# Final norm and delta-layer norm: x times both weights as the projections' operand, token factors applied at the projections' evictions

## The reference, cut to what matters

```python
# end of the first block
x = x + gt2[:, None, :] * y              # y: output of the experts
x = rmsnorm(x, g_final)                  # x * rsqrt(mean(x*x) + eps) * g
# start of the second block (h is x)
h = h + deltanet_mixer(rmsnorm_2(h, a_norm[i]), a_w_in[i], a_conv_w[i], ...)

def deltanet_mixer(h, w_in, conv_w, A_log, dt_bias, onorm_g, w_out):
    p = h @ w_in                         # 1024 -> 3072 (q, k, v) + 1024 (gate) + 16
    qkv, gate, b_raw, a_raw = jnp.split(p, [...], axis=-1)
    qkv = jax.nn.silu(causal_dwconv_2(qkv, conv_w))     # 4 taps along the tokens
    q, k, v = jnp.split(qkv, [A_QK, 2 * A_QK], axis=-1)
    q = l2norm(q.reshape(...)) * (A_DK ** -0.5)
    k = l2norm(k.reshape(...))
    beta = jax.nn.sigmoid(b_raw)
    g = -jnp.exp(A_log) * jax.nn.softplus(a_raw + dt_bias)
    o = gated_delta_rule_chunked(q, k, v, beta, g)
    o = rmsnorm_2(o, onorm_g) * jax.nn.silu(gate)
    return o @ w_out
```

## Time and profile before

| | |
|---|---|
| runs of the kernel | 2513.53, 2516.08, 2520.11 us; median 2516.08 |
| profiled execution | 2513.93 us, span 2512.2 us |
| busy share of the span | TensorE 91%, VectorE 48%, ScalarE 32%, GpSimd 5% |
| transposes of the expert sum start | 1084.48 us |
| tile 0 of the projections | 1135.59 us |
| first matmul of the delta rule | 1341.25 us |
| the casts of `wab`, VectorE (L2069, L2070) | 0.22 and 0.29 us, at 1105.23 |
| first two units of weights, issued at 1066.2 and 1066.7 | land after 15.0 and 19.4 us |
| a unit of weights (2 MB), median of 63 | lands after 8.1 us |

### The profile page before, as it was taken

How to read it: one execution, slowest core, us unless ns; L and a number is a source line. 1 busy time by engine, 2 the same in 40 slices (tenths; PEclk the granted TensorE clock), 3 DMA queues, 4 the chain that set the end, 5 groups by cost and what they waited for, 6 DMA issues and landing times.

```text
span 2512.2 us, 29683 instructions
## 1 busy us (share of the span) xinstructions
PE 2288.1 (91%) x11716; PEld 1574.4 (63%) x11716; DVE 1193.6 (48%) x1734; ACT 813.6 (32%) x1250; POOL 119.8 (5%) x160
## 2 busy tenths in 40 slices
PE   7999898599999999839988589999999889999997
PEld 3778656333333333317767577888787777888775
DVE  4889575300000000055645544777824473777832
ACT  4222452311111111143365164232324274223322
POOL 0000000111111111100002000000000000000000
PEclk9999999799999999969989599999999899999999
DMA  9442205449999999521110001222222301222221
GB/s 368 159 167 76 91 1 235 167 188 376 373 380 396 392 386 380 216 121 68 67 67 34 1 34 67 101 100 100 101 89 79 134 1 67 101 100 86 81 101 67
DMA packets 36405, 384.54 MB, mean 153 GB/s; under 512 B 10080, under 2 KB 10336, under 8 KB 13408
## 3 DMA queue, kind: packets, MB, share of 16 engines
q1 hardware_dynamic: 27520, 374.91, 38.1%
q0 software_dynamic: 8800, 8.45, 1.0%
HBM read 384.10 MB, written 16.83 MB: 160 GB/s over the span
## 4 chain that ended last, share of the span: by engine, by line
PE 55%; DVE 16%; ACT 5%; issue 3%; DMA 1%; DVEq 0%; POOL 0%; ACTq 0%; SPq 0%; POOLq 0%
PE PS L591 9%; PE PS L592 9%; PE PS L593 9%; PE PS L793 9%; PE PS L832 4%; PE PS L813 4%; DVE ring_r L2039 3%; PE PS L840 2%; DVE A L1755 2%; ACT w_hi_r L1378 2%; PE PS L557 2%; DVE A L2249 1%; DVE hid_r L2262 1%; DVE sq L2247 1%; DVE A L2250 1%
## 5 line engine op out<-in xcount | busy, mean ns | idle before, releaser
L592 PE MATMUL PS<-h_r,w_hi_r 128*128 128x512 f32 x1104 | 432.5, 392 | 0.0
L591 PE MATMUL PS<-h_hi_r,w_hi_r 128*128 128x512 f32 x1056 | 417.8, 396 | 10.6 <-ACT A L1405 7.2
L593 PE MATMUL PS<-h_hi_r,ring_r 128*128 128x512 f32 x1056 | 413.5, 392 | 0.0
L2039 DVE TENSOR_TENSOR ring_r<-ring,w_hi_r 128x1024 fp32r<-128x1024 f32 x196 | 238.6, 1223 | 361.7 <-ACT w_hi_r L1378 361.7
L1378 ACT ACTIVATE w_hi_r<-ring 128x1024 fp32r<-128x1024 f32 x196 | 202.6, 1051 | 331.2 <-PE PS L593 204.2
L591 PEld LDWEIGHTS PS<-h_hi_r,w_hi_r 128*128 128x128 f32 x1056 | 199.7, 189 | 62.6 <-issue 17.4
L592 PEld LDWEIGHTS PS<-h_r,w_hi_r 128*128 128x128 f32 x1104 | 209.1, 189 | 45.0 <-issue 1.9
L593 PEld LDWEIGHTS PS<-h_hi_r,ring_r 128*128 128x128 f32 x1056 | 199.5, 189 | 42.0
L2015 DVE TENSOR_TENSOR A<-A,PS 128x512 f32<-128x512 f32 x16 | 11.0, 688 | 395.2 <-PE PS L793 395.2
L793 PE MATMUL PS<-A 128*64 128x512 f32 x768 | 169.2, 597 | 0.1
L591 PE MATMUL PS<-x_r,top_r 128*128 128x512 f32 x320 | 129.0, 403 | 12.6 <-DVE ring_r L1665 12.6
(11 more groups left out here) (447 smaller groups left out, 3741.6 us busy)
## 6 DMA issues: line engine op xcount, KB each, us to landing
A<-wexp SPq DMA_DIRECT2D x64, 2048.0 KB, 12.5
ring<-wall SPq DMA_DIRECT2D x63, 2048.0 KB, 8.1
ring<-wexp SPq DMA_DIRECT2D x16, 2048.0 KB, 18.8
h<-wexp SPq DMA_DIRECT2D x16, 2048.0 KB, 13.3
A<-wada SPq DMA_DIRECT2D x12, 2048.0 KB, 13.5
x<-xt_in SPq DMA_DIRECT2D x2, 2048.0 KB, 11.3
A<-y_assignments SPq DMA_DIRECT2D x4, 1024.0 KB, 7.9
h_tokens<-A SPq DMA_DIRECT2D x4, 512.0 KB, 2.8
```

The source lines that it names most:

```text
L591: mm(out, w[0], x_[0], start=first, stop=False)
L592: mm(out, w[0], x_[1], start=False, stop=False)
L593: return mm(out, w[1], x_[0], start=False, stop=last_)
L2039: tt(ring_r[:, slot, :, cols], ring[:, slot, :, cols], w_hi_r[:, :, cols].bitcast(F32), ALU.subtract).then_inc(S("w_lo"), 1)
```

## The change

The projections' operand becomes x times both norms' weights, g_final and a_norm, without any factor of the token. It is split into high part (ScalarE) and low part (VectorE) tile by tile, right as x is updated. Both norms' factors are per token, so they can be applied to the projections' outputs: `token_scale` is the product of norm 3's factor and norm 2's, and every output tile is multiplied by it when it leaves PSUM. For q, k and v that is one multiply into SBUF ahead of the convolution, which then reads SBUF; for the gate tiles VectorE multiplies and ScalarE applies Silu in place; for the 16 gate values it takes the place of a copy. Norm 2 still writes x, and norm 3 still takes its squares from that x. TensorE does tile 0, the gate values' product, norm 2's sums, tiles 1 and 2, norm 3's sums, tile 3. The sums go to banks 5 and 6. ScalarE and VectorE do the weight pieces and norms in the same order. The split of `wab` moves ahead of the update of x.

```diff
--- before.py
+++ after.py
@@ -89,7 +89,7 @@
 
 GROUPS = ([([f"in{i}"], "A") for i in range(10)] + [(["conv_out"], "D")] * 2 + [(["m_out"], "D")] * 2
           + [(["w_out0"], "X"), (["w_out1"], "X")]
-          + [([f"a_in{i}"], "D" if i < 6 else "A") for i in range(8)] + [(["a_out0"], "X"), (["a_out1"], "X")]
+          + [([f"a_in{i}"], "D") for i in range(8)] + [(["a_out0"], "X"), (["a_out1"], "X")]
           + [([f"up0_{i}"], "D") for i in range(FU)] + [([f"down0_{3 * m + i}" for i in range(3)], "X") for m in range(2)]
           + [(["kv"], "D"), (["w_q0"], "D"), (["w_q1"], "D"), (["w_o0"], "X"), (["w_o1"], "X")]
           + [([f"up1_{i}"], "D") for i in range(FU)] + [([f"down1_{3 * m + i}" for i in range(3)], "X") for m in range(2)])
@@ -276,6 +276,7 @@
         o_sum, o_std = [sb(f"o_{n}", [P, NT, DH]) for n in ("sum", "std")]
         l_sum = [A[:, u, :] for u in (24, 25, 26, 27, 28, 29, 54, 55, 56, 57, 58)] + [rstd[:]] + [A[:, u, :] for u in (24, 25, 26, 27)]
         g_last = ab[:, :, 0:DH]
+        token_scale = A[:, 23, :]
 
 
         moe_up, moe_dn = [A[:, 0:8], A[:, 32:40]], [A[:, 24:32], h[:]]
@@ -527,7 +528,7 @@
             for u in range(UIDX["down1_0"], NU):
                 load(u)
 
-            sp.wait_ge(S("h"), 32)
+            sp.wait_ge(S("h"), 24)
             sp.dma_start(out_t, h[:]).then_inc(S("out"), 16)
             sp.wait_ge(S("out"), 16)
 
@@ -847,8 +848,6 @@
                 for t in range(NT):
                     last = nc.tensor.transpose(PS[:, k, t * P:(t + 1) * P], A[:, 16 + 2 * t + k // 4, (k % 4) * P:(k % 4 + 1) * P], ident)
                 last.then_inc(S("yT"), 1)
-            norm(2, 0)
-
 
             def w_split(slot, k, cols):
                 return w_hi_r[:, k, cols], ring_r[:, slot, k, cols]
@@ -903,14 +902,26 @@
                     last.then_inc(S("mm"), 1)
 
 
-            norm(3, 0)
-            wait_split(1)
-
+            def a_tile(j):
+
+                pe.wait_ge(S("w_lo"), split_count(NU1, j))
+                for k in range(KD):
+                    if j == 0:
+                        pe.wait_ge(S("h_lo"), KD * (1 + MIX_SETS) + k + 1)
+                    last = product(PS[:, j, :], w_split(unit_slot(UNITS[NU1]), k, slice(j * P, (j + 1) * P)), h_split(k), k == 0, k == KD - 1)
+                last.then_inc(S("mm"), 1)
+
+            a_tile(0)
             for k in range(KD):
                 last = product(PS[0:2 * DH, 4, :], (wab_hi[:, k, :], wab_lo[:, k, :]), h_split(k), k == 0, k == KD - 1)
             last.then_inc(S("ab_mm"), 1)
-            sgroup(G_AIN, h_split)
+            norm(2, NORM_BANK[2])
+            a_tile(1)
+            a_tile(2)
+            norm(3, NORM_BANK[3])
+            a_tile(3)
             pe.wait_ge(S("ab_ev"), 1)
+            pe.wait_ge(S("std"), 4)
             for t in range(NT):
                 last = nc.tensor.transpose(PS[:, 7, 16 * t:16 * t + 16], ab_rows[:, t * P:(t + 1) * P], ident[0:2 * DH, 0:2 * DH])
             last.then_inc(S("ab_mm"), 1)
@@ -1195,8 +1206,7 @@
                         act.wait_ge(S("sq_used"), KD * n + k - 1)
                     a_(sq[:, k % 2, :], x[:, k, :], ACT.Square).then_inc(S("sq"), 1)
                 act.wait_ge(S("sq_used"), KD * (n + 1))
-                bank = NORM_BANK[n]
-                inv_sqrt(rstd[:], PS[:, bank, :], 0, 1.0 / D).then_inc(S("std"), 1)
+                inv_sqrt(token_scale if n == 3 else rstd[:], PS[:, NORM_BANK[n], :], 0, 1.0 / D).then_inc(S("std"), 1)
 
             act.wait_ge(S("small"), 32)
             act.wait_ge(S("eps"), 5)
@@ -1366,7 +1376,6 @@
                     for half in range(2):
                         last = a_(yb[1][:, half, :], PS[HALF * half:HALF * (half + 1), 5, :], ACT.Copy)
                     last.then_inc(S("m_y1"), 1)
-            norm(2)
 
 
             def w_hi(u, j, load_count=None, free_count=None, slot=None):
@@ -1392,10 +1401,16 @@
                         act.wait_ge(S("h_free"), free + k + 1)
                     a_(dst[:, k, :], x[:, k, :], ACT.Identity, scale=V(gain_name, first + k)).then_inc(S("h_hi"), 1)
 
+            for k in range(KD):
+                act.wait_ge(S("xt"), KD + k + 1)
+                a_(h_hi_r[:, k, :], x[:, k, :], ACT.Identity, scale=gm[:, 0, k:k + 1]).then_inc(S("h_hi"), 1)
+                if k == 5:
+                    w_hi(NU1, 0)
+            w_hi(NU1, 1)
+            norm(2)
+            w_hi(NU1, 2)
             norm(3)
-            for j in range(4):
-                w_hi(NU1, j)
-            h_hi("h", KD * 3)
+            w_hi(NU1, 3)
 
             def sum_out(i):
 
@@ -1442,8 +1457,9 @@
                 for j in range(4):
                     if g == 6:
                         w_hi(NU1 + 7, j)
-                    act.wait_ge(S("mm"), TILE_DONE[G_AIN + g][j])
-                    a_(A[:, 16 + 4 * (g - 6) + j, :], PS[:, 4 * ((G_AIN + g) % 2) + j, :], ACT.Silu).then_inc(S("ev_act"), 1)
+                    act.wait_ge(S("ev_dve"), EMPTIED[G_AIN + g][1] - 3 + j)
+                    u = A[:, 16 + 4 * (g - 6) + j, :]
+                    a_(u, u, ACT.Silu).then_inc(S("ev_act"), 1)
                     if g == 6 and j == 0:
                         for i in range(8, 16):
                             act.wait_ge(S("l_ev"), i + 1)
@@ -2006,6 +2022,7 @@
             nc.vector.memset(dl[5][:], 0.0).then_inc(S("m_y0"), 1)
             nc.vector.memset(dl[4][:], 0.0).then_inc(S("m_y1"), 1)
             nc.vector.memset(A[HALF:P, 48, :], 0.0)
+            link(tt(gm[:, 0, :], V("g_final", 0, KD), V("a_norm", 0, KD), ALU.mult))
             n = doubles(dve)
 
             with dve.Fori(0, n) as d:
@@ -2024,12 +2041,23 @@
                 yy = A[:, 16 + 2 * t:18 + 2 * t, :].rearrange("p a b -> p (a b)")
                 link(ts(yy, y2[:, D:2 * D], wtok[:, 1, t:t + 1], None, ALU.mult))
                 stt(yy, y2[:, 0:D], wtok[:, 0, t:t + 1], yy, ALU.mult, ALU.add).then_inc(S("y_sum"), 1)
+            dve.wait_ge(S("small2"), 112)
+            link(cp(wab_hi, wab[:]))
+            link(tt(wab_lo, wab[:], wab_hi.bitcast(F32), ALU.subtract))
+
+            def a_lo(k):
+
+                dve.wait_ge(S("h_hi"), KD * (1 + MIX_SETS) + k + 1)
+                stt(h_r[:, k, :], x[:, k, :], gm[:, 0, k:k + 1], h_hi_r[:, k, :].bitcast(F32), ALU.mult, ALU.subtract).then_inc(S("h_lo"), 1)
+
             for k in range(KD):
                 dve.wait_ge(S("yT"), k + 1)
                 stt(x[:, k, :], PS[:, k, :], mod[:, 40 + k:41 + k], x[:, k, :], ALU.mult, ALU.add).then_inc(S("xt"), 1)
-
-            norm(2, V("g_final", 0, KD), x, "xt")
-
+                if k:
+                    dve.wait_ge(S("xt"), KD + k)
+                    a_lo(k - 1)
+            dve.wait_ge(S("xt"), 2 * KD)
+            a_lo(KD - 1)
 
             def w_lo(u, j, count=None, slot=None):
 
@@ -2065,15 +2093,16 @@
                 h_sets[0] += 1
 
 
-            dve.wait_ge(S("small2"), 112)
-            link(cp(wab_hi, wab[:]))
-            link(tt(wab_lo, wab[:], wab_hi.bitcast(F32), ALU.subtract))
-            norm(3, V("a_norm", 0, KD), h, "h")
-            for j in range(4):
-                w_lo(NU1, j)
-            h_lo()
+            h_sets[0] += 1
+            w_lo(NU1, 0)
+            w_lo(NU1, 1)
+            norm(2, V("g_final", 0, KD), x, "xt")
+            w_lo(NU1, 2)
+            dve.wait_ge(S("std"), 4)
+            link(tt(token_scale, token_scale, rstd[:], ALU.mult))
             dve.wait_ge(S("ab_mm"), 1)
-            cp(ab_rows, PS[0:2 * DH, 4, :]).then_inc(S("ab_ev"), 1)
+            tt(ab_rows, PS[0:2 * DH, 4, :], token_scale[0:2 * DH, :], ALU.mult).then_inc(S("ab_ev"), 1)
+            w_lo(NU1, 3)
             for m in range(24):
                 g = G_AIN + m // 4
                 if m == 4:
@@ -2094,17 +2123,26 @@
                 w_lo(NU1 + 1 + m // 4, m % 4)
                 dve.wait_ge(S("mm"), TILE_DONE[g][m % 4])
                 dst = A[:, m if m < 16 else 30 + m, :]
-                src = PS[:, 4 * (g % 2) + m % 4, :]
-                conv(dst, src, 4, lambda j: V("a_conv_w", 24 * j + m), None).then_inc(S("ev_dve"), 1)
+                z = A[:, 16 + m % 2, :]
+                link(tt(z, PS[:, 4 * (g % 2) + m % 4, :], token_scale, ALU.mult))
+                conv(dst, z, 4, lambda j: V("a_conv_w", 24 * j + m), None).then_inc(S("ev_dve"), 1)
                 if m in (20, 21):
                     for i in range(4 * (m - 20), 4 * (m - 20) + 4):
                         dve.wait_ge(S("l_r"), i + 1)
                         stt(A[:, i, :], A[:, i, :], float(P) ** -0.5, l_sum[i], ALU.mult, ALU.mult).then_inc(S("l_n"), 1)
+            def gate(i):
+
+                dve.wait_ge(S("mm"), TILE_DONE[G_AIN + 6 + i // 4][i % 4])
+                tt(A[:, 16 + i, :], PS[:, 4 * ((G_AIN + 6 + i // 4) % 2) + i % 4, :], token_scale, ALU.mult).then_inc(S("ev_dve"), 1)
+
             for j in range(4):
                 w_lo(NU1 + 7, j)
+                gate(j)
             for i in range(8, 16):
```

(4 more changed lines are left out.)

## The result

| | median us | runs | ratio to before |
|---|---|---|---|
| before | 2516.33 | 2513.53 to 2525.64 (5) | |
| changed | 2538.18 | 2537.64 to 2542.51 (5) | 1.0081, 95% interval 1.0063 to 1.0098 |

The changed kernel is slower by 21.9 us by the medians (15.9 to 24.7 by the interval of the ratio); the forecast was 2534, its range 2520 to 2542. The profiled execution took 2538.18 (span 2536.2), 24.3 more than the profiled one of before.

The account below looks back on a forecast made before the run. The prediction took a closed ring of ScalarE and VectorE, not TensorE, as the bound. Start +6.7, turns +10.6 and end +1.7 made +19.0 us, 2532.9 from the profiled execution or 2535 from the median; forecast 2534, range 2520 to 2542.

Parts of the forecast that it names:

- The ring: Projection tiles: ScalarE and VectorE wait for each other every tile, 6.37 us a turn, against 6.34 on TensorE.
- Rival 1: Projection turns: VectorE's 2.13 us of idling hides the added scaling; only start and end count, +8.4, 2522; chance 0.08.
- rival 2: Projection stage: TensorE sets the end after all, 1 to 5 us gained, 2509 to 2513; chance 0.07.
- The turn, 0.46: Each q, k, v tile: added scaling 0.72, multiply from SBUF 0.26 less, net 0.46; 23 turns, 10.6 us.
- wab, 1.3: Ahead of the update of x: VectorE's split waits for wab's late load, costing 1.3 us.
- The start, +6.7: From the update of x through both norms to turn 1: the ring starts 6.7 us later than before.
- Turn 1: Second turn of the ring, after the first Silu: forecast to start at 1153.9, before at 1147.20.
- 1.7 charged twice: TensorE's low clock after idling: 1.7 us charged at tile 0 and again at tile 2.
- my 12.5: Tile 0 and the gates' product on TensorE: forecast from 1099.1 to 1111.6.
- The end, +1.7: Gate tiles 24 to 31: Silu waits for w_lo and scaling, 1.5 shows, plus 0.2 for the last gate.
- The delta rule "unchanged in length": Delta rule after the projections: claimed to keep its length, no cost.
- rival 3: Projection stage: waits in every tile halve TensorE's clock, tiles take 10 us, +27 on top, 2560; chance 0.05.

Follow-up runs that it names:

- turn_only: Kernel before, plus one VectorE multiply by ones from PSUM into SBUF in each of the 24 turns, convolution reading SBUF: ratio 1.0070, 2536.23 us.
- before_ahead: Kernel before, with ScalarE rounding the next turn's weight piece ahead of this turn's Silu, no work added or dropped: ratio 0.9968.
- wab_later: Changed kernel, with the split of wab behind the first w_lo instead of ahead of the update of x: 2542.49 us, a single execution.
- start_only: Changed kernel without the multiply by the token factor for the 24 q, k and v tiles, convolution reading PSUM: ratio 1.0064.
- after_ahead: Changed kernel, with ScalarE rounding the next turn's weight piece ahead of this turn's Silu: ratio 0.9935, 2501.55 us.
- pieces_first: Changed kernel, with the first unit's four weight pieces rounded and subtracted ahead of norm 2 instead of between the norms: ratio 1.0054.
- copy_act: Changed kernel, with the delta rule's 128 x 8 copy of the decay's last column on ScalarE instead of VectorE: ratio 1.0068.

## Why the prediction was right

**The ring is the bound: right.** The turn's length before and after, VectorE's unchanged 2.13, and the fall of 16.6 us for a mere change of order in the kernel before show it. Rival 1 (hidden) and rival 2 (TensorE) are out: turn_only settles the first, before_ahead the second.

**The turn, 0.46: right.** 10.7 for the 23 distances of 24 Silu, forecast 10.6. The multiply from SBUF took 0.48 or 0.49, the three multiply-adds 2.32 against 2.31 from PSUM, so these return nothing. The table of cycles in the Trainium skill's page "VectorE: DVE Perf Modes" (section "The TRN2 errata — SBUF-src ops pay a fixed extra latency per instruction") gives 62 cycles fewer for an SBUF source; the estimate from it was 0.065 less for each multiply-add and 0.27 for the turn; the trace does not agree, and the measurement decides.

**wab, 1.3: right.** The update of x starts 2.57 behind the expert sum against 1.27 before, and wab_later brings it back to 1.28.

**The start, +6.7: a term was mis-sized.** Turn 1's w_hi came at 1155.86 for 1153.9, 8.7 later than before. The mechanism held at every mark; against 24 matmuls 0.227 apart the low clock cost 2.7 at tile 0 and 2.7 at tile 2, for 1.7 charged twice. The row I took the price from the earlier trace rows was one case of a spread: start_only and after_ahead show 12.6 and 12.5 for tile 0 with the product, right at my 12.5. How near the forecast comes is therefore in part luck of the execution. That the pieces of weight stood behind the scaling of x in VectorE's queue is what made norm 3 late, as pieces_first shows: its sums come 6.7 earlier after norm 2's.

**The end, +1.7: right** (1.8).

**The delta rule "unchanged in length": wrong by 2.4.** It is not a cost of the change's work. In the ten profiles whose code there is the same, the stretch is 38.6 in four and 40.9 to 41.4 in six. Up to the 32 matmuls of the third round all ten agree within 0.03 us, and they part at TensorE's granted clock there, after the same wait of 1.86: in the four it fell (the 32 matmuls take 5.47), in the six it stayed at 1.00 (3.84). Only in the six does GpSimd start early enough to hold up the copy, and there it is the fourth round that runs at half clock (6.3 to 6.8 for 3.84). So both have a part, 1.3 the copy and 1.1 TensorE's clock; copy_act takes away the first and still has a slow fourth round (5.47). Why the clock fell in the third round of some profiles and not of others is not known.

**The forecast of 2534** was 1.0 us above the sum on its own execution, and the median came 4 higher. The terms missed were those two: 2.0 of clock at the start and 2.4 of the delta rule. The chances do not follow from their own sizes: 0.80, 0.05 and half of 0.08 make 0.89 for slower, where 0.87 stands.

**The clock in the stage** (rival 3): over turns with a wait of 0.26 to 0.29 in each it stayed at 1.00, as the row below shows. It did not stay so everywhere: after a wait of 6.23 us ahead of 1194.60, which I had not foreseen, it was 0.51 over the next 5.4 us, and near the stretches with Ln and Exp it fell in both kernels. That cost no turn: the distances of the Silu are those before plus 0.46 there too, since the ring and not TensorE set them.

```profile
1218.77:1272.45 53.68, 51.53 (x207) 38.28 (x208) 36.53 (x48) 19.63 (x32) 0.00 (x0) 1.00 0.19 73
```

**Left open:** why ratios and stage sums differ by up to 5 us (start_only +16 by its ratio, +11.0 by its stage). The expert loop's end and the part behind the transpose vary from run to run; what in them varies was not tried.

## What to carry to other kernels

Before pricing an instruction by an engine's idle time, ask what that idle time waits for: when two engines wait for each other once per tile, every instruction of either lies on the path, and the busiest engine (here TensorE at 98%) merely has a lead that hides it. Such a ring is opened by order alone, by issuing the next tile's first link ahead of this tile's last; then the added work was free and the earlier start worth its full length. And an edit that moves a consumer forward can bring out a wait for a transfer: wab was issued last, and nothing had waited for it until its consumer moved.

## What the runs showed of the hardware that was not expected

A VectorE copy of 128 x 8 from SBUF, 0.16 us by itself, lasted 1.77 and 1.47 and ended 0.02 to 0.03 after a GpSimd multiplication; a VectorE multiplication of two SBUF tiles of 128 x 30, 0.20 us at that place in the kernel before, took 1.03 in the changed one, while VectorE instructions with one input in PSUM ran at their usual 1.22 beside GpSimd. The Trainium skill has this in "SBUF — State Buffer", section "SBUF: two separate sides": the port pair that VectorE and GpSimd share is locked by one of them for a whole instruction, and the other waits. The trace agrees in the two copies, which end with GpSimd's instruction. What it means here is that the same code has lengths that differ by 2.4 us, and that a faster TensorE in the third round goes with a longer stretch, in ten profiles of ten, though no run changed TensorE's pace alone.

The same wait of TensorE, 1.86 us at the same place of the same code, was followed by a lowered granted clock in four profiles (0.55 to 0.65) and by 1.00 in the six others with that code. And the same tile with the same product took 12.5 to 13.7 us after an idle TensorE, 11.14 with work ahead of it: the price of a low clock is a range, not a number.
